# Attention inside a decoder-trunk kernel: the four partial score sums are added down to two on VectorE before the matmuls with the values

## What is computed

```python
G = jnp.cumsum(g, axis=2)
...
A = jnp.einsum('nhtd,nhsd,nhtsd->nhts', q, k, decay)
o = jnp.einsum('nhts,nhsv->nhtv', A, v) + jnp.einsum('nhtd,nhdv->nhtv', q * jnp.exp(G), S)
...
S_new = jnp.exp(G_last[:, :, 0, :])[..., None] * S + jnp.einsum('nhsd,nhsv->nhdv', k * jnp.exp(G_last - G), v)
```

## Time and profile before

| | |
|---|---|
| time, median of 3 runs | 2971.77 us (2966.53 to 2972.17) |
| the profiled execution | 2968.65 us, its span 2966.9 us |
| PE busy | 2722.0 us, 92% of the span |
| DVE busy | 1186.6 us, 40% |
| ACT, POOL busy | 667.8 us, 432.2 us |
| attention loop, blocks 1 to 3 | some 84 us each |

### The profile page before, as it was taken

How to read it: one execution, slowest core, us unless ns; L and a number is a source line. 1 busy time by engine, 2 the same in 40 slices (tenths; PEclk the granted TensorE clock), 3 DMA queues, 4 the chain that set the end, 5 groups by cost and what they waited for, 6 DMA issues and landing times.

```text
span 2966.9 us, 36212 instructions
## 1 busy us (share of the span) xinstructions
PE 2722.0 (92%) x13095; PEld 2229.6 (75%) x13095; DVE 1186.6 (40%) x2344; ACT 667.8 (23%) x1335; POOL 432.2 (15%) x316
## 2 busy tenths in 40 slices
PE   5986697999999999889999998989999998899997
PEld 4865665888886778768887787778877787788776
DVE  6534834121112565832222476522224647322224
ACT  2201312111112223321112232121123223211123
POOL 3420513333334500200000002000000002000000
PEclk9975897898889999999999999999999999999999
DMA  4642024444456665135556562155555641355553
GB/s 147 204 152 65 15 86 151 170 174 171 173 181 211 226 256 193 40 138 185 195 185 220 186 243 84 64 187 189 187 218 186 234 176 44 142 184 191 193 215 135
DMA packets 142288, 489.05 MB, mean 165 GB/s; under 512 B 8896, under 2 KB 75696, under 8 KB 92967
## 3 DMA queue, kind: packets, MB, share of 16 engines
q1 hardware_dynamic: 133689, 482.64, 45.3%
q10 hardware_dynamic: 8472, 4.75, 0.6%
HBM read 375.52 MB, written 112.02 MB: 164 GB/s over the span
## 4 chain that ended last, share of the span: by engine, by line
PE 75%; DVE 6%; issue 4%; ACT 2%; DMA 0%; DVEq 0%; ACTq 0%
PE ps L483 24%; PE ps L485 24%; PE ps L484 24%; PE ps L611 1%; DVE arena L1563 1%; PE ps L637 1%; ACT arena L923 1%; DVE arena L1531 1%; DVE h_lo L1285 0%; DVE x_tok L1625 0%; DVE arena L1530 0%; DVE arena L1277 0%; PE ps L515 0%; DVE x_tok L1328 0%; ACT h_hi L940 0%
## 5 line engine op out<-in xcount | busy, mean ns | idle before, releaser
L483 PE MATMUL ps<-h_hi,w_both 128*128 128x512 f32 (+1 forms) x2240 | 853.5, 381 | 18.8 <-DVE x_tok L1625 8.9
L485 PE MATMUL ps<-h_lo,w_both 128*128 128x512 f32 (+1 forms) x2240 | 848.1, 379 | 0.0
L484 PE MATMUL ps<-h_hi,w_both 128*128 128x512 f32 (+1 forms) x2240 | 845.9, 378 | 0.0
L483 PEld LDWEIGHTS ps<-h_hi,w_both 128*128 128x128 f32 x2240 | 437.9, 196 | 101.1 <-issue 21.4
L484 PEld LDWEIGHTS ps<-h_hi,w_both 128*128 128x128 f32 x2240 | 437.6, 195 | 84.1
L485 PEld LDWEIGHTS ps<-h_lo,w_both 128*128 128x128 f32 x2240 | 437.1, 195 | 84.5
L483 PE MATMUL ps<-w_both,act_hi 128*128 128x512 f32 (+1 forms) x748 | 301.2, 403 | 27.0 <-DVE act_lo L1696 26.9
L485 PE MATMUL ps<-w_both,act_hi 128*128 128x512 f32 (+1 forms) x748 | 299.2, 400 | 0.0
L484 PE MATMUL ps<-w_both,act_lo 128*128 128x512 f32 (+1 forms) x748 | 298.5, 399 | 0.0
L1696 DVE TENSOR_TENSOR act_lo<-arena,act_hi 128x512 fp32r<-128x512 f32 (+1 forms) x176 | 135.4, 773 | 340.9 <-ACT act_hi L1173 340.9
L318 POOL TENSOR_TENSOR arena<-arena 128x256 f32<-128x256 f32 x56 | 40.5, 723 | 1513.2 <-DVE arena L1531 1513.2
(11 more groups left out here) (227 smaller groups left out, 2713.6 us busy)
## 6 DMA issues: line engine op xcount, KB each, us to landing
w_both<-w_split SPq DMA_DIRECT2D x288, 1024.0 KB, 4.8
w_split<-w_both SPq DMA_DIRECT2D x96, 1024.0 KB, 6.1
w_raw<-in_w_down SPq DMA_DIRECT2D x24, 512.0 KB, 4.1
w_raw<-in_w_a SPq DMA_DIRECT2D x22, 512.0 KB, 4.3
w_raw<-in_w_b SPq DMA_DIRECT2D x22, 512.0 KB, 4.3
w_raw<-in_w_in SPq DMA_DIRECT2D x20, 512.0 KB, 4.4
x_tok<-in_x_prompt SPq DMA_DIRECT2D x16, 512.0 KB, 6.7
arena<-in_x_prompt SPq DMA_DIRECT2D x16, 512.0 KB, 6.4
```

What stands on the lines that cost most here:

```text
L483: nc.tensor.matmul(out, lhs[0], rhs[0], start=first, stop=False)
L484: nc.tensor.matmul(out, lhs[1], rhs[0], start=False, stop=False)
L485: return nc.tensor.matmul(out, lhs[0], rhs[1], start=False, stop=last)
```

## The change

VectorE adds once more, in place: the second half of `a_sum` to its first half, after a wait for the first add. `outputs` then runs two matmuls with v, not four. `own.loop` has its count of marks raised by the 16 new ones of a block.

```diff
@@ outputs(i), TensorE
-                    for l in range((1 + LEVELS) // 2):
+                    for l in range((1 + LEVELS) // 4):
                         nc.tensor.matmul(o, a_sum[:, win(l)], v_tok[:, w, hc], start=l == 0, stop=False)
@@ masked(i), VectorE
-                    v.tensor_tensor(a_sum, a_all[:, 0:4 * P], a_all[:, 4 * P:8 * P], ALU.add).then_inc(at_ready, 1)
+                    own.mark(v.tensor_tensor(a_sum, a_all[:, 0:4 * P], a_all[:, 4 * P:8 * P], ALU.add))
+                    own.settle()
+                    v.tensor_tensor(a_sum[:, 0:2 * P], a_sum[:, 0:2 * P], a_sum[:, 2 * P:4 * P], ALU.add).then_inc(
+                        at_ready, 1)
@@ the loop over blocks 1 to 3, VectorE
-            with own.loop(1, BLOCKS, 106) as b:
+            with own.loop(1, BLOCKS, 122) as b:
```

## The result

The changed kernel takes **2981.91 us**, the median of 6 runs (2980.24 to 2984.25), against 2969.67 of 6 runs of the kernel before (2966.53 to 2972.17). The ratio is 1.0042, with a 95% interval of 1.0029 to 1.0055: slower by 12 us, as forecast (2980, range 2973 to 2988). The profiled execution took 2982.89 us, its span 2981.1.

What follows compares the result with a forecast made beforehand. VectorE was taken to bound steps 3 to 9, TensorE the steps before, both in turn after; three blocks at +7.6 and block 0 at +2.2 make +9.8 us on a mean of 2969.8: 2980 us, range 2973 to 2988.

Steps and rivals of the forecast that it cites:

- The middle steps: Steps 3 to 9, blocks 1 to 3: VectorE has no gap, so each costs +0.46 us (4.88 instead of 4.42), together +3.22.
- Rival 2: Every step: VectorE's wait for its first add costs nothing, a step gains 0.34 us, the total is 2974 us; chance 0.07.
- Two more savings: Steps 1 and 2, blocks 1 to 3: TensorE bounds and idles cover the adds, -0.90 us, making -1.18 when operands begin.
- The start: First outputs of blocks 1 to 3: +0.17 us for the new add, -0.45 for its matmuls, together -0.28.
- The tail: Steps 10 to 15 of blocks 1 to 3, followed wait by wait: together +0.51 us.
- step 11: In blocks 1 to 3 +0.46 us, after -0.44 from earlier outputs; in block 0, at half clock, 0.85 us given back.
- the last outputs: End of a block's loop: +0.46 us, waiting for the gate behind the last new add, and -0.45 for fewer matmuls.
- Rival 4: TensorE's clock falls to half in the 28 operand steps, +0.7 us each, 19 us more, 2999 us; chance 0.05.
- The prediction's own sign of being wrong: Middle part of block 3's loop: the forecast is wrong if the granted clock there is below 1.
- VectorE's wait of 0.93 disappears: Near the end of block 3's loop, VectorE's wait before L1569 at 2500.55 goes: -0.90 us.
- Block 0: First block, without u tiles: start, operand steps, later steps and weight split together +2.2 us.
- the split: GpSimd's splitting of weights beside steps 10 and 11 of block 0: new adds may meet it, 0 to 4.2 us, taken as 0.4.

Runs made afterwards that it cites:

- no_wait: Changed kernel, but in blocks 1 to 3 the second add reads the mask's products, so needs no wait; two partial sums left out: 2978.43 us, ratio 1.0035 to before.
- late_add: Changed kernel with VectorE's second add moved behind the state update and the gate: 2979.64 us, ratio 1.0033 to the kernel before.
- mm_only: Kernel before with two matmuls with v instead of four and no second add, two partial sums left out: 2962.42 us, ratio 0.9977.
- add_only: Changed kernel with the second add written to a scratch and still four matmuls with v: 2984.7 us, ratio 1.0065 to the kernel before.
- act_order: Changed kernel with ScalarE, in blocks 1 to 3, copying the next step's keys ahead of the u tile: 2977.12 us, a single run.
- some_steps: Kernel before with late second add and two matmuls only on steps where TensorE sets the pace, plus keys copied before u tile: 2955.86 us, ratio 0.996.
- warm: Changed kernel with TensorE issuing a small product two times more ahead of step 13: 2985.13 us, ratio 1.0062 to the kernel before.

## Why the prediction was right, and where it was not

**The middle steps: right.** +0.46 a step was forecast, 4.88 us measured. 0.12 of it is the wait (no_wait, late_add) and 0.34 the add. Seven steps gave +3.20 (forecast 3.22). That VectorE bounds there is shown from both sides: mm_only leaves the step at 4.42, add_only at 4.88. Rival 2 is out: the Trainium skill ("VectorE: DVE Perf Modes", section "The DRAIN you can't avoid") has a semaphore between two operations as costing nothing extra. Here the measurement decides otherwise: no_wait, without it, is 0.12 us a step faster, in each of seven steps.

**"Two more savings", steps 1 and 2: failed.** This term said -0.28 - 0.90 = -1.18 when the operands begin; the masks show -0.54. I took the eight instructions of L637 for all that could hold TensorE between the sums and the state, and did not look who releases L643. It needs L1064's keys, which are queued on ScalarE behind a u tile's copy of 0.58 us. TensorE now arrives first and waits 0.26 us, in both steps. The start gave 0.33 (forecast 0.28), but then a step's saving of 0.45 came to 0.10 on TensorE, twice, and that is the whole difference: act_order takes the wait away, and TensorE is 0.69 us earlier at step 3, of which 0.41 reaches VectorE.

**The tail: right but for the clock.** +0.51 was forecast from step 10 to the end. Where the clock held it came true term by term: in act_order's block 2, against the kernel before, step 10 gives +0.47, step 11 +0.03 (forecast 0.46 - 0.44), steps 12 and 13 +0.45 and +0.46, and the last outputs -0.89 (forecast -0.89). In the changed kernel -0.54 at the operands' begin, +3.20 and +0.52 would be the 87.69 of a loop without a fall; then the clock adds 1.17. Rival 4, which I gave 0.05, came true at one place in a block, and not at the one that I priced. The Trainium skill ("TensorE: Matmul & The Clock Gate", "A second HAM failure mode: psum-queue depth-cycling") tells of another kernel whose clock oscillated because of micro-idles between groups of matmuls. The changed kernel's rows agree, in the middle part too:

```profile
2479.00:2483.00 4.00, 2.97 (x25) 2.75 (x24) 3.96 (x6) 1.78 (x5) 2.80 (x4) 1.00 0.00 0
2483.00:2487.00 4.00, 3.13 (x19) 3.11 (x20) 3.93 (x10) 1.38 (x5) 2.33 (x4) 0.75 0.00 0
```

The prediction's own sign of being wrong, a granted clock below 1 in the middle part, thus came up (0.90). What I had wrong was the chance and the price. I let the clock fall for all 28 steps and bound them at 5.6 us each. It falls for about one step at a time, twice among the seven middle steps of each block, and in the middle part the idle ahead of it also pays for it: TensorE's slow matmuls fill the slack, and VectorE goes on at 4.88. In the timeline of TensorE's matmuls, a slow step and the next:

```profile
2465.96 2.68 PE L611 MATMUL ps<-arena 128*128 128x128 f32 x14
2468.79 0.30 PE L624 MATMUL ps<-tab,arena 128*128 128x128 f32 x1
2469.01 0.68 PE L637 MATMUL ps<-arena 128*128 128x128 f32 x4
```

L611 ran at half the clock and ended at 2468.64, just as VectorE's state update let L624 go: nothing was lost. Only in step 13, where VectorE has nothing else to do and waits for the scores, does a fall reach the end.

**"VectorE's wait of 0.93 disappears", and the last outputs: right where the clock holds.** In act_order's block 2, without the fall, L1571 (the first sum there) starts 1.24 us after the last mask, without a wait. In the changed kernel it still waits 0.49 us for the outputs; this and the 0.64 of the last mask make up 1.13 of the 1.17. The last outputs follow the new add and the gate (L637 after a wait of 1.22 us for L1586), where before it was 1.18 for the gate.

**Block 0: too low, at the start and in step 11.** Forecast +2.2, measured +4.04 in the first pair of profiles and +2.77 in the second. When the operands begin (mask 4) the shift is +0.71 in the first pair and -0.32 in the second, where I had -0.3. That is mostly the clock: from mask 1 to mask 2, where the granted clock was 0.61 before and 0.50 after, it took 5.42 and 5.89 us in the two profiles of the kernel before, 5.48 and 5.13 in the changed one and 4.86 in no_wait, which has the same instructions there as the changed one. The seven steps 3 to 9 then add 3.93, of which 3.2 was forecast, and step 10 adds 0.05 instead of 0.46. These two are the split's (VectorE and GpSimd):

```profile
359.62 1.48 POOL L459 TENSOR_SCALAR w_both<-w_raw 128x1024 fp32r<-128x1024 f32 x1
360.23 1.14 DVE L1571 TENSOR_TENSOR arena<-arena 128x256 f32<-128x256 f32 x1
...
368.78 2.66 POOL L462 TENSOR_TENSOR w_both<-w_raw,w_both 128x1024 fp32r<-128x1024 f32 x1
369.16 1.21 DVE L1563 TENSOR_TENSOR arena<-ps,tab 128x1024 f32<-128x1024 f32 x1
370.40 1.59 DVE L1569 TENSOR_TENSOR arena<-arena 128x512 f32<-128x512 f32 x1
371.42 1.48 POOL L459 TENSOR_SCALAR w_both<-w_raw 128x1024 fp32r<-128x1024 f32 x1
372.03 1.14 DVE L1571 TENSOR_TENSOR arena<-arena 128x256 f32<-128x256 f32 x1
...
373.54 1.21 DVE L1563 TENSOR_TENSOR arena<-ps,tab 128x1024 f32<-128x1024 f32 x1
```

Both new adds met the split and took 1.14 us, 0.7 more than alone. Yet steps 9 and 10 together grew from 14.21 to 15.44 us, by 1.23, where 2 x 0.46 and the 0.4 that I allowed for the split make 1.32. The allowance held, and for its stated reason: an add that meets GpSimd ended a fixed time after GpSimd's instruction. The two L1571 of 128x256 end 0.27 us after their L459, the L1569 of 128x512 0.55 after its L462. In step 10 the first add took 2.70 us before and 1.59 after, so that the new one found its place in time that VectorE had lost anyway.

What failed is step 11, at half clock. I had -0.85 for it (half a clock, four instructions fewer). From mask 12 to mask 13, before and after (windows):

```profile
364.73:370.52 5.79, 5.77 (x31) 5.78 (x32) 2.37 (x5) 0.64 (x3) 2.88 (x2) 0.59 0.00 0
```

```profile
373.54:379.21 5.67, 5.64 (x27) 5.66 (x28) 2.79 (x6) 0.63 (x3) 1.85 (x1) 0.52 0.01 3
```

TensorE has no gap in either, and it did four instructions fewer, but the clock stayed low for longer (0.52 against 0.59), so only 0.12 us came back; in the second pair it was 0.66. Steps 12 and 13, with -0.35 forecast for each, gave -0.45 and -0.06: together 0.51 of 0.70, as the new step is 2.79 and then 3.18 us instead of 2.89 twice.

**The sum.** The loops came to +17.1 instead of +9.8: the start of blocks 1 to 3, most of it the late keys (3 x 0.64 = 1.9), the clock in step 13 (3 x 1.17 = 3.5) and block 0 (1.8) make up the difference of some 7.2. The total is nevertheless only +12.2 in the medians. In the first pair of profiles stretches outside attention gave back 2.9 us (4.1 more ahead of the first mask, 5.9 less behind block 0's loop, 1.1 less in the rest), in the means of two pairs next to nothing (loops +16.5, spans +16.3). That the forecast came within 2 us is thus in part luck: the main term was right, the missing ones were +7, and between the medians some 5 us of it do not appear. Where those went is not shown, as only one of the six executions behind each median left a trace. The sentence "after attention TensorE bounds again, so the delay is passed on whole" was too simple: passed on, but blurred by falls of the clock that came in some executions and not in others.

## What to carry to other kernels

Before work is moved from one engine to another, ask in each stretch which engine has no gap, and apply the change only there: a saving of 0.45 us a step on TensorE against 0.46 on VectorE makes the loops 17 us longer when it is made in every step, and, with the two reorderings, 5.4 us shorter when it is made only in the steps where TensorE is the one without a gap. If an operation must wait for its predecessor on its own engine, put independent work between them: the same result then costs only its slot. And when a path gets shorter, look at every other input of its next instruction; here a copy on ScalarE that had always come in time became the wait.

## What the runs showed of the hardware

- A semaphore wait of VectorE on its own previous instruction costs 0.12 us, and behind two other instructions (0.45 us of slots) nothing: 4.88 against 4.76 us a step.
- TensorE's granted clock fell behind the idle of 2.80 us in step 13 in all six such steps seen of the changed kernel (two profiles), and in none behind 1.84 us (before, some_steps; two profiles each), 1.88 (mm_only), 2.27 (late_add), 2.54 (no_wait) or 1.08 (warm). But the length of the idle alone does not decide: behind the same 2.80 us it fell in only one of act_order's three blocks, behind 2.76 in one of add_only's three, and behind the 3.2 us wait ahead of FFN down in some profiles and not in others. Stretches with and without such a fall differed by 1 to 4 us, on a kernel where the edit itself was to move 10.
- With one idle filled by two products that nobody needs (warm) the clock stayed up there, and in two of three blocks fell at the next idle. A fall on an engine that another one keeps waiting cost nothing (4.88 us a step with it and without); it has to be judged by who waits behind it.
- An operation of VectorE with both inputs in SBUF that starts while GpSimd works on SBUF ends a fixed time behind GpSimd's instruction, whatever that one is: 0.27 to 0.29 us behind for 128x256, 0.54 to 0.56 for 128x512, in all 73 such cases in and around the attention loops of blocks 0 and 3, in one trace of each of the two kernels. So a 128x256 add, 0.41 us alone, took 0.83 us beside an add of GpSimd and 0.80 to 2.56 beside a part of the split, by how much of that part was still to come.
